# The gated delta stage of a two-block layer: raw keys in channel order, with the key norm and beta moved into per-partition factors

## The reference, cut to what matters

```python
q, k, v = jnp.split(silu(causal_depthwise_conv(qkv, w_conv_qkv)), 3, axis=-1)
q, k, v = l2norm(heads(q)), l2norm(heads(k)), heads(v)      # x * rsqrt(sum(x*x) + EPS)
beta = sigmoid(b_raw)
g_log = -exp(a_log) * softplus(a_raw + dt_bias)
...
gc = cumsum(g_log)                                          # per head, within a chunk
decay = exp(where(causal, gc_i - gc_j, -inf))
A = (beta_i * k_i . k_j) * decay * strict                   # 16 heads
T = inverse(I + A)
v_new = T (v * beta) - T (k * beta * exp(gc)) S             # S: state of 128 x 128 per head
o = (q * exp(gc)) S + (q k^T * decay) v_new
S = S * exp(gc_last) + (k * exp(gc_last - gc))^T v_new
```

## Time and profile before

| what | value |
|---|---|
| median of 3 runs | 2748.7 us |
| the profiled execution's own time | 2749.76 us |
| its span in the trace | 2748.1 us |
| PE busy | 2690.1 us, 98% of the span |
| PE weight load busy | 2341.3 us, 85% |
| DVE busy | 1700.1 us, 62% |
| ACT busy | 1252.8 us, 46% |
| POOL busy | 166.2 us, 6% |
| DMA | mean 180 GB/s, hardware queue 53.7% of 16 engines |

### The profile page before, as it was taken

How to read it: one execution, slowest core, us unless ns; L and a number is a source line. 1 busy time by engine, 2 the same in 40 slices (tenths; PEclk the granted TensorE clock), 3 DMA queues, 4 the chain that set the end, 5 groups by cost and what they waited for, 6 DMA issues and landing times.

```text
span 2748.1 us, 40906 instructions
## 1 busy us (share of the span) xinstructions
PE 2690.1 (98%) x14658; PEld 2341.3 (85%) x14658; DVE 1700.1 (62%) x2216; ACT 1252.8 (46%) x1513; POOL 166.2 (6%) x338
## 2 busy tenths in 40 slices
PE   8999999999999999999989999999999999999997
PEld 7888888888888888888888989898998999878886
DVE  5555555555455555554566566464889898866564
ACT  5444444444444444444455545353444444364453
POOL 0000000000000000000004040313000000000000
PEclk9999999999999999999999999999999999999999
DMA  7555555555555555555645453544555555556654
GB/s 253 177 183 177 180 177 177 181 179 190 191 189 192 191 191 188 190 201 193 195 135 169 149 173 118 171 142 155 171 190 194 183 194 183 173 179 193 225 172 143
DMA packets 150275, 495.28 MB, mean 180 GB/s; under 512 B 28528, under 2 KB 29264, under 8 KB 149648
## 3 DMA queue, kind: packets, MB, share of 16 engines
q1 hardware_dynamic: 147664, 482.77, 53.7%
q0 software_dynamic: 2496, 10.87, 1.2%
HBM read 490.42 MB, written 3.16 MB: 180 GB/s over the span
## 4 chain that ended last, share of the span: by engine, by line
PE 89%; POOL 3%; DVE 2%; DMA 2%; issue 1%; ACT 1%; SPq 1%; DVEq 0%; ACTq 0%; POOLq 0%
PE PS L1511 22%; PE PS L1513 22%; PE PS L1512 22%; PE PS L1525 5%; PE PS L1527 5%; PE PS L1528 5%; PE PS L1687 2%; POOL xt L477 2%; POOL xi L481 1%; PE PS L1536 1%; PE PS L1694 0%; DVE wlo L911 0%; ACT whi L537 0%; DMA iT<-diag_in 0%; PE PS L1706 0%
## 5 line engine op out<-in xcount | busy, mean ns | idle before, releaser
L911 DVE TENSOR_TENSOR wlo<-raw,whi 128x1024 fp32r<-128x1024 f32 x900 | 1099.5, 1225 | 987.3 <-ACT whi L537 982.5
L537 ACT CAST whi<-raw 128x1024 fp32r<-128x1024 f32 x900 | 943.3, 1051 | 1359.4 <-PE PS L1513 1024.1
L1511 PE MATMUL PS<-whi,aH 128*128 128x512 f32 x1792 | 702.6, 392 | 2.3 <-DVE wlo L911 1.7
L1512 PE MATMUL PS<-wlo,aH 128*128 128x512 f32 x1792 | 698.1, 390 | 0.0
L1513 PE MATMUL PS<-whi,aL 128*128 128x512 f32 x1792 | 698.1, 390 | 0.0
L1525 PE MATMUL PS<-aH,whi 128*128 128x256 f32 x1536 | 442.9, 288 | 1.5 <-DVEq L1309 1.4
L1528 PE MATMUL PS<-aH,wlo 128*128 128x256 f32 x1536 | 437.5, 285 | 2.5 <-issue 2.5
L1527 PE MATMUL PS<-aL,whi 128*128 128x256 f32 x1536 | 437.6, 285 | 0.0
L1511 PEld LDWEIGHTS PS<-whi,aH 128*128 128x128 f32 x1792 | 336.9, 188 | 72.6 <-DVE wlo L911 2.9
L1513 PEld LDWEIGHTS PS<-whi,aL 128*128 128x128 f32 x1792 | 336.8, 188 | 70.4
L1512 PEld LDWEIGHTS PS<-wlo,aH 128*128 128x128 f32 x1792 | 337.1, 188 | 68.2
(11 more groups left out here) (292 smaller groups left out, 2236.2 us busy)
## 6 DMA issues: line engine op xcount, KB each, us to landing
raw<-in_stream SPq DMA_DIRECT2D x900, 512.0 KB, 3.3
H<-in_x SPq DMA_DIRECT2D x4, 512.0 KB, 7.8
pB<-in_pool_b POOLq DMA_DIRECT2D x4, 512.0 KB, 3.8
dT<-cum_rows SPq DMA_DIRECT2D x8, 256.0 KB, 4.1
iT<-diag_in SPq DMA_DIRECT2D x16, 128.0 KB, 3.4
bg<-in_b_gate POOLq DMA_DIRECT2D x8, 256.0 KB, 4.0
out<-eb SPq DMA_DIRECT2D x4, 512.0 KB, 2.9
dmask<-in_dmask POOLq DMA_DIRECT2D x1, 1536.0 KB, 10.0
```

The source lines that it names most:

```text
L537: nc.scalar.copy(whi[:, s], raw[:, s]).then_inc(hi_done, 1)
L911: nc.vector.tensor_tensor(wlo[:, s], raw[:, s], whi[:, s].bitcast(F32), ALU.subtract).then_inc(lo_done, 1)
L1511: mm(out, hi[:, kt + k, tok], whi[:, s, k], start=kt + k == 0, stop=False)
L1512: mm(out, hi[:, kt + k, tok], wlo[:, s, k], start=False, stop=False)
```

## The change

In the reference the unknowns are v_new. The change solves for w = v_new * norm / beta instead, with norm = sqrt(sum(k*k) + EPS) of the raw key. Then the raw key k, as the convolution leaves it in channel order, stands in every product, and one factor per token of the source, beta / norm^2, is left. That token lies on the partition in `aT`, `qk` and `ke`, so the factor is a per-partition scalar of the instruction that multiplies by the decays anyway. The right side becomes v * norm (`gk`) in place of v * beta, and the state's share is scaled by -exp(gc) (`necum`) in place of -beta * exp(gc). In detail:

- `kn`, `kb`, `knT`, `kbT` are gone, with ACT's 8 scalings and 2 copies, DVE's 8 scalings, and PE's 16 transposes of a group. `st` gets its own buffer.
- Right behind the turn of the key PE multiplies the raw key with itself: after chunk 11, after chunk 12 in group 0. The turn now also waits for `o1s_sb`.
- 1/norm^2, beta/norm^2 and its negative are made by DVE (`key_scales`, 4 operations on 8 columns); POOL keeps one operation, the square root (`gk`).
- `aT` is 8 operations of 128 columns instead of one of 1024, in step 12 (13 in group 0) instead of 15. `ke` follows in step 13 and reads the turned key in PSUM banks 6 and 7, so PE's transposition of the last group's output now waits for `ke_sb`. `qk` is 8 operations of 128 columns too.
- SP's steps of the inverse come earlier: 12, 15 and 16 instead of 14, 17 and 18.
- `LV` is 33 instead of 34, so the whole late part comes one chunk earlier.
- In group 0 the decay rows are no longer read back from DRAM: PE makes them after chunk 11 by 8 matmuls of `cumT` with a column of the unit matrix, DVE reads them from PSUM banks 6 and 7 in step 11, and the turn after chunk 12 waits for that.

The diff, cut to its core and moved 12 columns to the left:

```diff
+LV = 33
 TRI, REC = 5, 5
...
-        if j == 14:
-            sp.wait_ge(kb_sb, i + 1)
+        if j == 12:
+            sp.wait_ge(sqn_sb, i * 2 + 1)
             sp.dma_start(xi[:], dram["eye"]).then_inc(xn_in, 16)
-        if j == 17:
+        if j == 15:
...
-        if j == 18:
+        if j == 16:
...
-    else:
-        pool.wait_ge(beta_sb, 1)
-    pool.wait_ge(sqn_sb, i * 2 + 1)
-    nc.gpsimd.tensor_scalar(eight(rk[:, 0]), eight(sqn[:, 0]), EPS, None, ALU.add).then_inc(rk_sb, 1)
-    pool.wait_ge(rk_sb, i * 3 + 1)
-    nc.gpsimd.tensor_tensor(eight(rk[:, 1]), eight(rk[:, 0]), mhalf[:, 0:8], ALU.pow).then_inc(rk_sb, 1)
-    pool.wait_ge(rk_sb, i * 3 + 2)
-    nc.gpsimd.tensor_tensor(rkb[:], rk[:, 1], beta[:, :, i * HG:(i + 1) * HG], ALU.mult).then_inc(rk_sb, 1)
-    pool.wait_ge(kt_ps, i + 1)
-    pool.wait_ge(ke_sb, i + 1)
+    pool.wait_ge(en_sb, i * 4 + 1)
+    nc.gpsimd.tensor_tensor(eight(gk[:]), eight(se[:]), half_up[:], ALU.pow).then_inc(gk_sb, 1)
+    if i:
+        pool.wait_ge(rec_ps, (i - 1) * REC + VN1)
...
-        if j == (14 if first else 8):
+        if j == (11 if first else 8):
             act.wait_ge(dt_sub, i + 1)
             nc.scalar.activation(dT[:], dT[:], ACT.Exp).then_inc(dt_sb, 1)
...
-        if j in (11, 21):
-            act.wait_ge(*((k_ps, i + 1) if j == 11 else (q_ps, i + 1)))
-            nc.scalar.activation(gm[:].rearrange("p t h n -> p t (h n)"), PS[:, 6:8] if j == 11 else PS[:, 4:6],
-                                 ACT.Square).then_inc(sq_sb, 1)
-        if j == 13:
-            act.wait_ge(rk_sb, i * 3 + 2)
-            for t in range(NT):
-                for h in range(HG):
-                    ins = nc.scalar.activation(kn[:, t, h], heads(6)[:, t, h], ACT.Copy,
-                                               scale=rk[:, 1, t, h:h + 1])
-                ins.then_inc(kn_sb, 1)
-        if j == 14:
-            copy_heads(knT, 4, kt_ps, kt_sb, i + 1)
-            copy_heads(kbT, 6, kt_ps, kt_sb, i + 1)
+        if j == (12 if first else 11):
+            act.wait_ge(k_ps, i + 1)
+            nc.scalar.activation(gm[:].rearrange("p t h n -> p t (h n)"), PS[:, 6:8], ACT.Square).then_inc(sq_sb, 1)
+        if j == 21:
+            act.wait_ge(q_ps, i + 1)
+            nc.scalar.activation(gm[:].rearrange("p t h n -> p t (h n)"), PS[:, 4:6], ACT.Square).then_inc(sq_sb, 1)
...
-def log_decays(i):
-    dve.wait_ge(dt_in, i * (16 * NT) + 16 * NT)
+def key_scales(i):
+    dve.wait_ge(sqn_sb, i * 2 + 1)
+    nc.vector.tensor_scalar(se[:], sqn[:, 0], EPS, None, ALU.add).then_inc(en_sb, 1)
+    dve.wait_ge(en_sb, i * 4 + 1)
+    nc.vector.reciprocal(rse[:], se[:]).then_inc(en_sb, 1)
+    dve.wait_ge(en_sb, i * 4 + 2)
+    group = beta[:, :, bass.ds(i * HG, HG)]
+    nc.vector.tensor_tensor(en[:, 0], rse[:], group, ALU.mult).then_inc(en_sb, 1)
+    nc.vector.scalar_tensor_tensor(out=en[:, 1], in0=rse[:], scalar=-1.0, in1=group, op0=ALU.mult,
...
+        if first and j == 11:
+            dve.wait_ge(ba_ps, 4)
+            log_decays(i, heads(6))
+        if not first and j == 6:
+            dve.wait_ge(dt_in, i * (16 * NT))
+            log_decays(i, dT)
...
+        if j == (13 if first else 12):
+            dve.wait_ge(dt_sb, i + 1)
+            dve.wait_ge(en_sb, i * 4 + 4)
+            nc.vector.tensor_tensor(ed[:], en[:, 0, 0], dT[:, 0, :, P - 1], ALU.mult).then_inc(ke_sb, 1)
+            dve.wait_ge(a_ps, i + 1)
+            for t in range(NT):
+                for h in range(HG):
+                    ins = nc.vector.scalar_tensor_tensor(out=aT[:, t, h], in0=heads(4)[:, t, h],
+                                                         scalar=en[:, 1, t, h:h + 1], in1=dT[:, t, h],
+                                                         op0=ALU.mult, op1=ALU.mult)
+            ins.then_inc(a_sb, 1)
         if j == 13:
-            dve.wait_ge(rk_sb, i * 3 + 3)
-            for t in range(NT):
-                dve.wait_ge(kn_sb, i * NT + (t + 1))
-                for h in range(HG):
-                    ins = nc.vector.tensor_scalar(kb[:, t, h], heads(6)[:, t, h], rkb[:, t, h:h + 1], None, ALU.mult)
-            ins.then_inc(kb_sb, 1)
-        if j == 15:
-            dve.wait_ge(a_ps, i + 1)
-            dve.wait_ge(dt_sb, i + 1)
-            nc.vector.scalar_tensor_tensor(out=aT[:].rearrange("p t h n -> p t (h n)"), in0=PS[:, 4:6], scalar=-1.0,
-                                           in1=dT[:].rearrange("p t h n -> p t (h n)"), op0=ALU.mult,
-                                           op1=ALU.mult).then_inc(a_sb, 1)
-        if j == 15:
+            dve.wait_ge(ke_sb, i * 2 + 1)
             for h in range(HG):
-                ins = nc.vector.tensor_scalar(ke[:, h], kn[:, 0, h], dT[:, 0, h, P - 1:P], None, ALU.mult)
+                ins = nc.vector.tensor_scalar(ke[:, h], heads(6)[:, 0, h], ed[:, h:h + 1], None, ALU.mult)
             ins.then_inc(ke_sb, 1)
         if 15 <= j <= 17:
             conv(i, 1, j - 14)
         if j == 21:
             norms(i, 1)
             dve.wait_ge(qk_ps, i + 1)
-            nc.vector.tensor_tensor(qk[:], heads(6), dT[:], ALU.mult).then_inc(qk_sb, 1)
+            for t in range(NT):
+                for h in range(HG):
+                    ins = nc.vector.scalar_tensor_tensor(out=qk[:, t, h], in0=heads(6)[:, t, h],
+                                                         scalar=en[:, 0, t, h:h + 1], in1=dT[:, t, h],
+                                                         op0=ALU.mult, op1=ALU.mult)
+            ins.then_inc(qk_sb, 1)
...
                skip_group_check=True).then_inc(ba_ps, 1)
-        if j == 11:
+        if first and j == 11:
+            pe.wait_ge(cum_sb, 3)
+            for t in range(NT):
+                for h in range(HG):
+                    n = t * DN_HEADS + h
+                    pick = con[0:2 * DN_HEADS, 0, n:n + 1].to_broadcast([2 * DN_HEADS, P])
+                    ins = mm(PS[:, 6 + t, h * P:(h + 1) * P], pick, cumT[:], start=h == 0, stop=True,
+                             skip_group_check=True)
+            ins.then_inc(ba_ps, 1)
+        if j == (12 if first else 11):
             pe.wait_ge(kqv_sb, i * 3 + 1)
-            if not first:
+            if first:
+                pe.wait_ge(dt_sub, 1)
+            else:
                 pe.wait_ge(o1_sb, i * (HG + 1))
+                pe.wait_ge(o1s_sb, i)
             turn(6, lambda t, h: kqv[:, 0, h, t * P:(t + 1) * P]).then_inc(k_ps, 1)
-        if j == 14:
-            pe.wait_ge(kn_sb, i * NT + NT)
-            if first:
-                pe.wait_ge(cum_sb, 3)
-            else:
-                pe.wait_ge(o1s_sb, i)
-            turn(4, lambda t, h: kn[:, t, h])
-            pe.wait_ge(kb_sb, i + 1)
-            turn(6, lambda t, h: kb[:, t, h]).then_inc(kt_ps, 1)
-        if j == 15:
-            pe.wait_ge(kt_sb, i * 2 + 2)
```

More of the change, by code:

```diff
@@ L47 @@
 ROWS = BLK // 4
-LV = 34
+LV = 33
 TRI, REC = 5, 5
@@ L692, in _ @@
             act.sem_inc(zb_sb, 1)
-            def copy_heads(to, bank, wait, after, value):
-                act.wait_ge(wait, value)
-                nc.scalar.copy(to[:].rearrange("p t h n -> p t (h n)"), PS[:, bank:bank + 2]).then_inc(after, 1)
             o = oD[:].rearrange("p t (h n) -> p t h n", h=HG)
@@ L1263, in delta @@
                         done(dve, q, j)
[L1264 removed]
+                    if first and j == 14:
                         dve.wait_ge(cum_sb, 4)
[L1266 to L1268 removed]
+                        nc.vector.tensor_scalar(necum[:], ecum[:], -1.0, None, ALU.mult)
+                    if j == (12 if first else 11):
@@ L1811, in delta @@
                         pe.wait_ge(a_sb, i + 1)
-                        if not first:
+                        if first:
+                            pe.wait_ge(ke_sb, 2)
+                        else:
                             pe.wait_ge(t_lo, i * QT + T_D * QT)
                         turn(4, lambda t, h: kqv[:, 1, h, t * P:(t + 1) * P]).then_inc(q_ps, 1)
-                        by_head(6, lambda t, h: knT[:, t, h],
+                        by_head(6, lambda t, h: kqv[:, 0, h, t * P:(t + 1) * P],
                                 lambda t, h: kqv[:, 1, h, t * P:(t + 1) * P]).then_inc(qk_ps, 1)
```

50 lines of the change are left out of this document (25 added, 25 removed).

## The result

The changed kernel is slower: 2776.2 us in the median of 4 runs (2764.5 to 2781.5) against 2749.2 for the kernel before on the same chip, a ratio of 1.0092 (95% interval 1.0067 to 1.0116). Forecast were 2741.0 us, and 0.06 for slower. The profiled execution is the fastest of the four, 2764.5 us with a span of 2762.8.

What follows compares the result with a forecast made beforehand. PE, busy 98% of the span, was taken to bound the kernel through its work, stops and clock. Terms -12.2 -6.8 -4.3 -2.6 +1.7 +1.3 +5.3 +9.9 = -7.7 us gave 2742.1 profiled, 2741.0 median; range 2732 to 2749.

Steps and rivals of the forecast that it cites:

- the likeliest case: Whole kernel: the forecast itself, 2741.0 us, with its own range 2737 to 2746 us and a chance of 0.50.
- Waits for normalised keys: Delta stage, PE: waits for normalised keys and the old SiLU stop of group 0 go, 12.2 us less.
- Transposes: Delta stage, PE: 16 transposes fewer per group, in 4 groups, 6.8 us less.
- Inverse: Delta stage, PE: waits for the transposed inverse fall from 7.7 to 3.4 us, 4.3 us less.
- Decay rows: Delta stage, group 0: 8 new float32 matmuls (16 instructions) on PE, 1.7 us more.
- `dT` in group 0: Delta stage, group 0: PE waits for `dt_sub` on DVE after the decay rows and chunk 12, 1.3 us more.
- SiLU after chunk 11: Delta stage, groups 1 to 3: PE waits 1.75 us each for ACT's SiLU of the key, 5.3 us more.
- Rival D: Stops after chunk 11: a function table change costs twice the row, stops some 3.0 us, total 2752.1 us; chance 0.05.
- `ke` after chunk 14: Delta stage, groups 1 to 3: PE waits 3.3 us each for `ke_sb` from DVE, 9.9 us more.
- Clock: Delta stage: low-clock loss falls from 9.8 to 7.2 us, one low stretch per `ke` stop, 2.6 us less.
- rival E: Groups 1 to 3: clock falls after chunk 11 and stays low until chunk 14, total 2757.5 us; chance 0.06.

Runs made afterwards that it cites:

- b_pad32: Kernel before plus an unused buffer of 32 bytes a partition where the change puts `half_up`: 2770.2 us, ratio 1.0080.
- a_again: The changed kernel run again without an edit, on the same chip as the other runs of its series: 2774.8 us, ratio 1.0097 to the kernel before.
- a_noshift: Changed kernel with `half_up` in unused columns of `epsilon`, so later buffers keep their addresses of before: 2755.2 us, ratio 1.0024 to the kernel before.
- b_fill208: Kernel before with 416 redundant PE waits (208 instructions) ahead of stage D's first transpositions: 2774.3 us, ratio 1.0090.
- a_fill64: a_noshift with 128 redundant PE waits (64 instructions) ahead of stage D's first transpositions: 2744.8 us, ratio 0.9981 to the kernel before.
- a_fill48: a_fill64 with 96 redundant PE waits (48 instructions) in place of 128: 2743.6 us, ratio 0.9984 to the kernel before.
- a_tail: a_fill64 with the tail of each group's recurrence (square, scaling, transposition of the output) one chunk later: 2727.7 us, ratio 0.9929 to the kernel before.
- b_front128: Kernel before with 128 unused bytes a partition ahead of all large buffers: 2747.5 us, ratio 0.9997.
- b_pad64: Kernel before plus an unused buffer of 64 bytes a partition where the change puts `half_up`: 2770.2 us, ratio 1.0080.
- b_pad128: Kernel before plus an unused buffer of 128 bytes a partition where the change puts `half_up`: 2766.3 us, ratio 1.0063.
- b_mid128: Kernel before with 128 unused bytes a partition between `wlo` and `H`, so `raw`, `whi` and `wlo` stay: 2791.1 us, ratio 1.0156.

## Why the prediction was wrong

**The step that failed is its first paragraph:** "only two things can move the time: work on PE, and the moments at which PE stands still or runs at a lower clock", followed by "The change touches the delta stage alone". The first sentence still holds if the length of one matmul counts as work. The second is false. The diff had two side effects outside the stage, and the sum has a term for neither:

- *Addresses, +20 us in the pitch (start to start) of 3072 matmuls* (`b_pad32` +22.1; `a_again` less `a_noshift` 19.6). `half_up` stood in the diff, and its consequence could have been read from the order of the buffers, though not its price: no row of before shows a displaced tile.
- *Place of G's loop in PE's program, +9 us* (G +9.1 in `a_noshift`; `b_fill208` G +10.9). The removed transposes, counted as a gain of 6.8 us, are also what moved it (32 fewer in the program, less the 8 new matmuls). A sign was there: queue 8 brings nothing in G's last two passes before the change, and I didn't ask on what that rested.

**The sum for stage D was right in its parts.** The side effects taken away, the change is a gain: `a_fill64` 0.19% and `a_fill48` 0.16% below before, 5.2 and 4.4 us, against 7.7 forecast and inside the likeliest case's range. That it is near the forecast is in part luck, since stage D gained between 3.5 and 11.8 us in the five executions that have the changed stage. Step by step, from the changed kernel's rows above:

- *Waits for normalised keys, -12.2:* gone, all of them.
- *Transposes, -6.8:* the 64 are gone; their price was not measured by itself.
- *Inverse, 3.4 us left:* 3.4 in 4 waits in the profiled execution, but 3.9 in `a_again` and `a_noshift` and 5.4 to 6.1 in `a_fill48`, `a_fill64` and `a_tail`, where PE no longer stops at the jump ahead of it. So that gain is not firm. SP's wait for POOL is gone.
- *Decay rows, 1.7:* 1.98, the row starting at 1456.20 and the next matmul at 1458.18.
- *`dT` in group 0, 1.3:* 0.90.
- *SiLU after chunk 11, 1.75:* 1.78. The fourth wait of that line, 0.69 us at 1491.7, belongs to the turn of the query in group 0, and the kernel before has it as well (0.69 us at 1482.6). Rival D's 3.0 us did not come: the drain that the Trainium skill, page "ScalarE: Activation LUTs", section "What ACT_TABLE_LOAD costs", puts on top of the table load isn't seen in this stop.
- *`ke` after chunk 14, 3.3:* 3.06.
- *Clock, -2.6:* this is where the executions differ. In the profiled one, only the first of the three stops for `ke` has a low stretch, and 3.3 us of busy time are lost from 1400 to 2000 us; D gains 11.8. In `a_again` 10.8 are lost there and D gains 3.5, with the same waits for `ke` and `kqv`; 3.5 of them stand behind one wait for the inverse, 2.14 us long for 0.89. The forecast gave each stop for `ke` a low stretch; over five executions 10 of 15 had one. No stop after chunk 11 of the profiled execution was followed by a low stretch, so rival E has no part in the loss.

The rest of the loss adds up roughly: -6.9 for D, +9.1 for G and +19.6 for the addresses make 21.8, and R took 2.1 more in `a_noshift` than in the trace before; among executions with the addresses of before it lies anywhere from 570.7 to 573.1. `a_again` measured 26.7. Of the difference I can say only that it lies within the spread of D.

## What to carry to other kernels

Look at a diff for what it does to addresses and to the length of the program, not only to the work. Here a buffer of 32 bytes cost 22 us and a program that is 32 instructions shorter cost 9, both in stages that the change didn't touch, and each more than what the change was worth. Compare the packets of the instruction queue before and after. Keep the two operands of large matmuls at the same address modulo 256 (here, pad small buffers together to a multiple of 256 bytes, or put them behind the large ones), and compare the duration of an untouched instruction before believing a sum of waits.

A step that was moved by one chunk creates stops on engines that share it. Two such stops, each foreseen by the chunk, were worth some 16 us once they were taken away, and that is more than the change itself gained in the delta stage.

## What the runs showed of the hardware

- A matmul of 512 columns (float32r, 128x128 stationary) starts every 227 ns when both operands start at the same address modulo 256 bytes (here 128, or 0 in `b_front128`), and every 231 to 236 (medians of the groups; 5 to 7 ns more in the mean, by `b_pad32`, `b_pad64`, `b_pad128` and `b_mid128`) when the stationary one lies 32, 64 or 128 bytes further. At 256 further it is 227 again. Other distances weren't tried. The 4608 with 256 columns, where the roles of the tiles are exchanged (`whi` stationary), have their operands moved apart in `b_mid128` alone, and stayed at 120 ns there. Why is open: the rows show the pace and not its cause.
- PE's instructions come in packets of 16 KB (queue 8 of the kernel before: 84 packets, 1.38 MB in its page). A packet holds 256 instructions. G's loop of 1582 ran without any new packet where it touches 7 such blocks and fetched 9 packets a pass where it touches 8; D's of 1781 or 1813 touches at least 8 everywhere and was always fetched. Starting 32 instructions earlier was enough to go from one to the other. In G a fetching pass stopped PE at the jump, 1.8 to 3.7 us, and behind 6 of 8 such stops in four executions the granted clock was low for a while (0.61 and 0.53 over 4 us in `a_noshift`). Where D's loop begins 63 or more instructions ahead of a border, it was fetched without a stop.
- 208 instructions of waits on a value already reached took PE's idle 8.2 us and 10.3 more, so they are not free; 64 of them made the same stop 0.2 us longer.
- The granted clock behind one and the same stop differs from execution to execution: the three stops for `ke`, of 3.06 us each, were followed by one low stretch in the profiled execution, by two in `a_again`, `a_noshift` and `a_fill48` and by three in `a_fill64`.
